# A list scheduler with a longer hand-over to TensorE, and other gates on the first weight loads

## What is computed

```python
h = rmsnorm(x, norm_mix_g)
proj = h @ w_in                       # q, f, i, g, c_gate, b_gate, xb, gate_a, gate_b
y_a = hgrn2_mixer(q_raw, f_raw, i_raw, g_raw, lb, hg_norm_g) @ w_branch_a
y_b = short_conv_mixer(c_gate, b_gate, xb, conv_w) @ w_branch_b
x = x + (sigmoid(gate_a) * y_a + sigmoid(gate_b) * y_b) @ w_out
x = x + swiglu(rmsnorm(x, norm_ffn_g), w_ffn_gate, w_ffn_up, w_ffn_down)
return rmsnorm(x, norm_final_g)

# hgrn2: f = lb + (1 - lb) * sigmoid(f_raw)  (forget gate),  value v = i_raw
# S_t = diag(f_t) S_{t-1} + (1 - f_t) v_t^T,   o_t = S_t^T (silu(q_t) * 128**-0.5)
```

## Time and profile before

| what | us |
|---|---|
| median of 3 runs | 1033.21 |
| lowest, highest | 1032.44, 1033.33 |
| the profiled execution | 1035.37 |
| its slowest core (core 3), first to last instruction | 1033.8 |
| the fastest core of that execution (core 2) | 1024.6 |
| PE busy in the slowest core | 1000.4 |
| DVE, ACT busy there | 470.1, 406.5 |

### The profile page before, as it was taken

How to read it: one execution, slowest core, us unless ns; L and a number is a source line. 1 busy time by engine, 2 the same in 40 slices (tenths; PEclk the granted TensorE clock), 3 DMA queues, 4 the chain that set the end, 5 groups by cost and what they waited for, 6 DMA issues and landing times.

```text
span 1033.8 us, 15076 instructions; the slowest of 8 cores (1024.6 to 1033.8 us)
## 1 busy us (share of the span) xinstructions
PE 1000.4 (97%) x5446; PEld 489.0 (47%) x5446; DVE 470.1 (45%) x666; ACT 406.5 (39%) x690; POOL 23.2 (2%) x49
## 2 busy tenths in 40 slices
PE   4799999999999999999999999999999999999997
PEld 4465545454555545444444444444444444444444
DVE  5686565476777776446564332121212121232223
ACT  3786553676767675233433231111111111111112
POOL 2000000000000000000000000000000000000000
PEclk9899999999999999999999999999999999999999
DMA  9973324024000261723329444020403116222211
GB/s 193 216 205 122 103 62 82 1 30 95 1 1 2 41 115 49 119 86 123 119 86 180 133 95 82 1 41 1 82 1 59 24 28 194 103 104 102 82 61 62
DMA packets 20232, 84.87 MB, mean 82 GB/s; under 512 B 2368, under 2 KB 2368, under 8 KB 16960
## 3 DMA queue, kind: packets, MB, share of 16 engines
q0 software_dynamic: 5904, 33.03, 18.5%
q1 hardware_dynamic: 14112, 50.62, 14.4%
q10 hardware_dynamic: 144, 0.26, 0.1%
HBM read 100.16 MB, written 16.78 MB: 113 GB/s over the span
## 4 chain that ended last, share of the span: by engine, by line
PE 89%; DMA 5%; issue 2%; DVE 2%; ACT 2%; SPq 0%; POOL 0%; ACTq 0%; DVEq 0%; POOLq 0%
PE pf L736 59%; PE pf L1304 15%; PE pf L745 10%; DMA arena<-x_main 2%; PE pf L763 2%; DMA ring<-x_prev 1%; DMA ring<-wall 1%; ACT arena L714 1%; PE pf L969 1%; PE pf L794 1%; DVE arena L863 1%; DVE arena L718 0%; PE pf L1122 0%; PE pf L829 0%; PE pf L1168 0%
## 5 line engine op out<-in xcount | busy, mean ns | idle before, releaser
L736 PE MATMUL pf<-hT,ring 128*128 128x512 bf16 x2560 | 573.5, 380 | 2.2 <-ACT arena L714 1.8
L736 PEld LDWEIGHTS pf<-hT,ring 128*128 128x128 bf16 x2560 | 249.4, 98 | 298.6 <-issue 4.1
L1304 PE MATMUL pf<-ring,arena 128*128 128x512 bf16 (+1 forms) x726 | 152.2, 373 | 0.0
L714 ACT ACTIVATE arena<-pf 128x512 f32<-128x512 f32 (+3 forms) x164 | 99.3, 641 | 102.7 <-PE pf L736 84.8
L714 ACT ACTIVATE rtmp<-pf 128x512 f32<-128x512 f32 (+1 forms) x89 | 52.8, 593 | 176.5 <-PE pf L736 176.4
L1304 PEld LDWEIGHTS pf<-ring,arena 128*128 128x128 bf16 x726 | 71.0, 98 | 81.2
L718 DVE TENSOR_TENSOR arena<-rtmp,pf 128x512 bf16<-128x512 f32 (+1 forms) x69 | 46.9, 679 | 134.8 <-PE pf L736 130.0
L745 PE MATMUL pf<-ring,arena 128*128 128x512 bf16 x384 | 92.6, 389 | 5.0 <-DMA ring<-wall 4.8
L736 PE MATMUL pf<-arena,ring 128*128 128x512 bf16 x320 | 79.7, 379 | 1.0 <-ACT arena L714 1.0
L714 ACT ACTIVATE rtmp<-hT 128x1024 bf16<-128x1024 f32 (+2 forms) x18 | 17.3, 962 | 123.7 <-DVE hT L718 123.7
L745 PEld LDWEIGHTS pf<-ring,arena 128*128 128x128 bf16 x384 | 37.9, 100 | 50.5 <-issue 10.2
(11 more groups left out here) (99 smaller groups left out, 667.8 us busy)
## 6 DMA issues: line engine op xcount, KB each, us to landing
ring<-wall POOLq DMA_DIRECT2D x25, 1024.0 KB, 10.7
ring<-x_prev SPq DMA_DIRECT2D x16, 512.0 KB, 6.9
ring<-x_main SPq DMA_DIRECT2D x16, 512.0 KB, 4.4
arena<-x_main SPq DMA_DIRECT2D x16, 512.0 KB, 4.6
x1spill<-arena SPq DMA_DIRECT2D x16, 512.0 KB, 2.9
hT<-x1spill SPq DMA_DIRECT2D x16, 512.0 KB, 3.6
out<-hT SPq DMA_DIRECT2D x15, 512.0 KB, 2.7
ring<-wall POOLq DMA_DIRECT2D x6, 512.0 KB, 6.5
```

Of the source, the lines that this page charges most:

```text
L714: P.op("act", lambda E: E.activation(out=rs(out), in_=rs(in_), func=func, **kw), reads=reads, writes=writes, dur=dur, aset=ASET[func] if f ...
L736: last = E.matmul(pb(bk)[:, 0:ncol], lhsT=sl[:, o_:o_ + 128], rhs=rhs[:, c, :], start=(c == 0), stop=(c == kc - 1))
L1304: last = E.matmul(pb(bk)[:, 0:w], lhsT=act_v(c)[:, n * 128:(n + 1) * 128], rhs=rl[c], start=(c == 0), stop=(c == 21))
```

## The change

Five edits, all in what sets the order; no arithmetic is changed.

1. The gates of the first loads: "f" has none, the four quarters of "i" wait for x tiles 1, 1, 2 and 2, and x tiles 4 to 7 wait for the four quarters of "i". x tiles 8 and later wait only for their buffer.
2. The scheduler counts an operation of PE as ready 0.8 us after what it needs on another engine, in place of 0.15 us.
3. DMA_RATE is 295 in place of 310 (thousand bytes per us).
4. `pick` lets an operation that is not the oldest of PE take banks only if an aligned free pair is left over (before: two free banks anywhere), and prefers a bank whose neighbour is in use. PE's oldest open operation is always among the candidates.
5. Estimated durations of eight transposes (0.7 to 0.48 us) and of the halo matmuls (2.0 to 0.9 us).

```diff
-DMA_RATE = 310.0e3
+DMA_RATE = 295.0e3
 DMA_LAT = 2.2
+PE_SLACK = 0.8
...
         def pick(n, oldest):
-            nfree = sum(1 for h in held if not h)
-            if nfree - n < (0 if oldest else 2):
-                return None
             best = None
...
+                if not oldest:
+                    rest = [h or k <= j < k + n for j, h in enumerate(held)]
+                    if not any(not rest[j] and not rest[j + 1] for j in range(0, nbanks, 2)):
+                        continue
                 t = max(bank_free[k:k + n])
-                if best is None or t < best[0]:
-                    best = (t, k)
-            return best
+                key = (t, n == 1 and not held[k ^ 1])
+                if best is None or key < best[0]:
+                    best = (key, k)
+            return None if best is None else (best[0][0], best[1])
...
+                if e == "pe" and head_pe < len(pend_pe) and pend_pe[head_pe] in avail[e] and pend_pe[head_pe] not in cand:
+                    cand.append(pend_pe[head_pe])
...
-                q.ready = max(q.ready, o.fin + (0.06 if q.eng == e else 0.15))
+                q.ready = max(q.ready, o.fin + (0.06 if q.eng == e else PE_SLACK if q.eng == "pe" else 0.15))
...
-        load_next([None, None, xm[0], xm[1]], 4)
-        load_next([xm[1], xm[2], xm[3], xm[3]], 4)
-        xgate.update({4: xm[3], 5: b_ring[slot_of["f"]][3]})
-        xgate.update({6 + q: b_ring[slot_of["i"]][q] for q in range(4)})
+        load_next([], 4)
+        load_next([xm[1], xm[1], xm[2], xm[2]], 4)
+        xgate.update({4 + q: b_ring[slot_of["i"]][q] for q in range(4)})
...
-            P.op("pe", tr, reads=[b_xs, b_ident], writes=[tb.buf], dur=0.7)
+            P.op("pe", tr, reads=[b_xs, b_ident], writes=[tb.buf], dur=0.48)
...
-                P.op("pe", fn, reads=b_sl + [b_hcol], writes=[bk.buf], dur=2.0)
+                P.op("pe", fn, reads=b_sl + [b_hcol], writes=[bk.buf], dur=0.9)
```

More of the change, by code:

```diff
@@ L893, in tr @@
                     return last
-                P.op("pe", tr, reads=[b_kT[kb], b_ident], writes=[tb.buf], dur=0.7)
+                P.op("pe", tr, reads=[b_kT[kb], b_ident], writes=[tb.buf], dur=0.48)
                 for q in range(2):
```

## The result

The changed kernel is slower. Both of its undisturbed executions took 1038.5 us (two further ones, of 1122.8 and 1201.9 us, had one die at a lower clock and are left out); the four of before that ran beside them took 1031.2 to 1033.3. The ratio is 1.0058, 95% interval 1.0034 to 1.0082. I had forecast 1030.2 us, with a range of 1026.8 to 1034.4.

What follows compares the result with a forecast made beforehand. PE 97% busy, the start bound by ACT and DVE plus lost clock in cores 3 and 6. Slowest core 6: 1032.2 - 1.1 - 2.0 = 1029.1, 4.7 us below core 3 before; median taken as 1030.2 us, range 1026.8 to 1034.4.

Steps and rivals of the forecast that it cites:

- The bound: Whole kernel: PE busy 97% of the span; the start bound by ACT and DVE, plus lost clock in cores 3 and 6.
- The gates of "f": First loads: ungating "f" costs and gives nothing, 0 us; each us that x tiles 1 to 3 are held up costs 1.
- Slab "i" at about 27 us, the wait of 4.84 at 0.5: Block 0's value matmuls: slab at about 27 us, not 31.3; 7.2 us less in core 3 with clock, 2.9 in core 1.
- the gates don't do what they say: Rival at the first loads: slab still lands near 31 us, time 1031.2; inside the forecast's range, no separate chance.
- The x tiles 4 to 7 are not late: Block 1's x loads: not delayed, since up to the last of them both queues move the same bytes as before.
- The chain of ACT and DVE: From x96 to block 2's forget products: 49.7 us in every core; -3.9 us in core 3, -1.1 in core 6, +2.0 in core 1.
- The hand-over and the bank rule: PE's order: work moves where PE waited, -2.0 us ahead of the second main block's convolution; no new gaps elsewhere, 0.
- my slower case: Rival: PE idles more between 34 and 47 us, every core gets the low clock; 1036 us, chance 0.16.
- The 1.84 us ahead of hT1: Ahead of the second main block's convolution: 16 more value matmuls (3.5 us) remove the wait, -2.0 us in every core with small ones.
- The low clock I expected between 34 and 47 us: PE thinly used from 34 to 40 us, between transposes behind DVE: 1.0 us added for low clock, bounds 0 to 3.5.
- The stop at 577 us: PE's 3.49 us wait in core 6 for an x tile sharing DMA with three slabs: stays as it was.

Runs made afterwards that it cites:

- only_slack: Kernel before with one edit, the hand-over time to PE of 0.8 us in place of 0.15: ratio to before 1.0034.
- fit_gates_x: Kernel before with DMA_RATE 250, hand-over 0.25 us, edit 5's durations, new gates, and x tiles 8 and 9 waiting for slab "i"'s last quarter: 0.9959.
- the good plan: Kernel before with DMA_RATE 250, hand-over to PE 0.25 us and the changed kernel's durations; gates and bank rule as before: ratio 0.9940, median 1027.9 us.
- slack_015: Changed kernel with the old hand-over time to PE, 0.15 us in place of 0.8: ratio to before 1.0005.

## Why the prediction was wrong, step by step

**The bound (right).** PE busy nearly all the time, nearly all differences in the first 150 us, and ACT and DVE the second bound behind the slab: the table bears it out in the main. The two kernels with the least idle time before 152 us are the fastest, and the one that never waits for the slab is no faster than they are. Idle time alone doesn't rank them all: only_slack has more of it than the changed kernel (13.3 against 12.4 us) and is faster.

**The gates of "f" (right as far as seen).** The x96 starts at 21.1 to 22.1 us in the eight cores, against 20.8 to 22.0 before.

**Slab "i" at about 27 us, the wait of 4.84 at 0.5 (wrong).** Measured: values from 29.8 us in the mean against 30.5 before, waits of 1.52 to 3.27 us, and the x32 partly at the low clock still in cores 3 and 7 (8.75 and 9.87 us). The step that failed is "x tile 4 is issued only when quarter 0 of "i" has landed, so its data flow from about 22 us on": that is so for tile 4, but tiles 8 and 9 were issued at 16 and 21 us. With 29.8 us the slab came nearer to my rival "the gates don't do what they say" (near 31) than to the forecast. With them gated (fit_gates_x) the values start at 27.1 us and the wait is 0.0. That the sum said 27 as well is in part luck: it let POOL's queue move 0.052 MB per us beside the x tiles, a mean over 11 us at whose end the queue had little left. In core 3 of fit_gates_x it moved 0.25 MB from 22 to 24 us beside tile 4, then 0.01 MB from 24 to 26, and the values began at 27.69 us.

**"The x tiles 4 to 7 are not late" (wrong), for the same reason.** Tile 4 lands at 31.3 us in core 3, 6 us later than before. In the trace of the changed kernel that makes ACT wait in core 7 alone (2.89 us). I had written that the two queues move the same bytes up to the last of them; they move 1 MB more.

**The chain of ACT and DVE, 49.7 us from the x96 to block 2's forget products (too low).** It was 50.5 to 55.3 us. In core 1, 51.1, the new stop of 3.30 us and 1.66 us of low clock behind it lie inside; less these it is 46.2, which is 3.5 us under my 49.7. So the total is too low by the stop, and the chain in it was put too high. What made the stop is the next step.

**The hand-over and the bank rule: "a scheduler that reckons with later results makes none, so 0" (wrong; the step that weighs most).** I took a longer hand-over to be a safe margin: it can only order work later than it is ready. But the list scheduler takes whatever can start first; every ready time that moves changes who goes first on PE, and through PE the order on ACT and DVE. At both new stops transposed x tiles stand behind two scans in DVE's order, and PE behind both. Alone the hand-over costs 0.34%, on top of the other edits 0.53%, and only in the first 150 us. It is not the whole: the bank rule and the gates make the stop at 65 us without it, and cost 0.33% in the kernel before (0.14 and 0.19%). The prices don't add up, and none is a price of the edit by itself. I gave this step 2 us of gain, and to a loss from it no rival at all: my slower case (16%) had 1036 us, but from the clock between 34 and 47 us.

**The rate and the durations (no term).** I put edits 3 and 5 at nothing and gave no reason. The one pair that differs in them alone shows 0.28%, and the rate alone gave 0.45% and 0.7% in other settings.

**The 1.84 us ahead of hT1 (wrong).** 16 value matmuls did move ahead of it, as the order shows, and PE waits 0.39 + 1.48 us all the same, for the last eight values and for DVE. Work put in front of a wait covers it only if what is waited for doesn't move back with it.

**The clock.** The low clock I expected between 34 and 47 us came in some cores (2.86 to 3.07 us for eight matmuls of 128x512 in cores 1, 4 and 5, against 1.89 in cores 2, 3 and 7), and again behind the new stops, where the eight matmuls next behind take 0.4 to 1.7 us longer.

**The stop at 577 us (nearly right).** 0.35 to 2.48 us, in every core; before 0 to 3.49, and the mean of the eight cores is 1.6 us in both.

**What stays open.** Why one order has stops and its neighbour (rate 245 or 250) hardly any is shown case by case, not explained by a rule. The gates cost 0.19 to 0.46% in three pairs; only in the good plan does holding tiles 8 and 9 back return most of it (0.27 of 0.46%), and that kernel has another order too.

## What to carry to other kernels

Where a scheduler sets the order, an edit of its numbers is a new order and has no price per edit: the same 0.8 us cost 0.34 and 0.53% in two settings and 0.16%, not clear of nothing, in a third, and 2% of a rate 0.7%. Read the times of the plan, not only its rows: both large stops stood in it. When a gate is moved, read the issuing queue's whole order with what each entry waits for: what lost its gate will go first. And a few kernels with neighbouring numbers, timed, are worth more than an argued one: one number (260 for 310) gave 0.45%.

## What the runs showed of the hardware that I had not expected

The low clock behind a stop is neither sure nor of one length. Behind the same stop of 2.46 or 2.47 us, in one execution, eight matmuls of 128x512 take 2.30 us in core 4 and 3.52 in core 1; in core 4 the next 16 then take 4.51 in place of 3.6. Core 4, after:

```profile
92.80 2.30 PE L749 MATMUL pf<-ring,hT 128*128 128x512 bf16 x8 [2.47 <-DVE hT L722]
...
95.75 4.51 PE L740 MATMUL pf<-hT,ring 128*128 128x512 bf16 x16
```

One stop can also leave the clock alone in one core and halve it in another: behind the same 3.20 us of only_slack the granted clock is 1.00 in core 6 and 0.53 in core 0 (from 95.6 to 98.6 us). Core 6, then core 0:

```profile
91.75 1.89 PE L746 MATMUL pf<-ring,hT 128*128 128x512 bf16 x8 [3.20 <-DVE hT L719]
...
95.51 3.31 PE L746 MATMUL pf<-ring,hT 128*128 128x512 bf16 x8 [3.20 <-DVE hT L719]
```

In fit_gates_x, core 1, a stop of 1.36 us is followed by eight at half speed throughout (3.57 us, the row above), but there the granted clock was at 0.50 already from 38.0 us on, behind 2.18 and 0.79 us of idle time and little work; behind the 2.50 us of slack_015 in core 1 sixteen run at full clock. The Trainium skill, "TensorE: Matmul & The Clock Gate", section "What's actually happening", has idleness lower the clock and activity lift it, not in phase with the kernel; the traces agree, and the loss can't be read off the stop's length.

POOL's queue moved 0.56 MB between 20.3 and 31.3 us beside 2.40 MB of x tiles (core 3, after), but that is no measure of how two queues share: it had little left after 26 us. Core 3, after, first 22 to 26 us, when both had work, then 26 to 31.3:

```profile
q0 software_dynamic: 230, 0.41, 61.5%
q1 hardware_dynamic: 165, 0.59, 42.6%
...
q1 hardware_dynamic: 442, 1.61, 90.0%
q0 software_dynamic: 31, 0.05, 6.6%
```

The Trainium skill, "DMA: Bandwidth & Descriptors", section "Queues, rings and completion order", says that each engine takes turns between its queues packet by packet. While both had work the packets stand at 230 to 165, near one to one but not at it; whether every engine had packets of both at each moment these counts don't show. And the slab was ready only when its last 31 packets were through: they took until past 28 us, and the value matmuls started at 29.48. A mean rate over the whole load, as I used it, hides both.
